# A hybrid decoder layer on one core: V and K products in eight steps of two K tiles, and modulation weights moved from the U products to the output projection

## The reference, cut to what matters

```python
m = silu(c) @ w_ada + b_ada              # 2048 x (6 * 2048): shift, scale, gate, shift2, scale2, gate2
h = rms_norm(x, g_pre) * (1.0 + scale) + shift
q, k, v, u = split(h @ w_in)             # 2048 -> 4 * 1024
attn   = diff_attend(rotary(q), rotary(k), v)        # samples also read pages of a cache
pooled = pool_mix(u)                     # window means minus u, times w_pool
mix = concat([rms_norm(attn) * 0.8, pooled]) @ w_out
x = x + gate * rms_norm(mix, g_post)
f = square(relu((rms_norm(x, g_pre2) * (1 + scale2) + shift2) @ w_ff1)) @ w_ff2
x = x + gate2 * rms_norm(f, g_post2)
```

## Time and profile before

| | us |
|---|---|
| median of 3 runs | 1502.26 (1497.86 to 1507.72) |
| the profiled execution | 1494.64 |
| its span, first to last instruction | 1493.0 |
| PE busy in the span | 1446.6 (97%) |
| DVE, ACT, POOL busy | 799.7, 517.5, 102.9 |
| first product matmul | 43.73 |
| first matmul of Q (fill 0) | 198.7 |
| first matmul of the output projection | 410.6 |

### The profile page before, as it was taken

How to read it: one execution, slowest core, us unless ns; L and a number is a source line. 1 busy time by engine, 2 the same in 40 slices (tenths; PEclk the granted TensorE clock), 3 DMA queues, 4 the chain that set the end, 5 groups by cost and what they waited for, 6 DMA issues and landing times.

```text
span 1493.0 us, 26969 instructions
## 1 busy us (share of the span) xinstructions
PE 1446.6 (97%) x10274; PEld 1313.3 (88%) x10274; DVE 799.7 (54%) x1258; ACT 517.5 (35%) x733; POOL 102.9 (7%) x177
## 2 busy tenths in 40 slices
PE   5999999999899998999999999999999999999996
PEld 1777777778588877999998999999999999999996
DVE  2655558856756568665334444333554344445554
ACT  2222233434456445333322333332333232333331
POOL 1000000067410000000000000000000000000002
PEclk9999999999999999999999999999999999999998
DMA  9999988889687777444445544445544444444431
GB/s 366 345 326 323 325 305 318 284 308 360 226 321 257 258 256 248 141 152 158 143 160 200 176 160 148 147 162 185 192 158 144 157 151 141 143 155 152 141 113 71
DMA packets 87880, 316.40 MB, mean 212 GB/s; under 512 B 12176, under 2 KB 12432, under 8 KB 87168
## 3 DMA queue, kind: packets, MB, share of 16 engines
q1 hardware_dynamic: 79200, 287.87, 56.1%
q0 software_dynamic: 5216, 22.51, 4.1%
q10 hardware_dynamic: 3392, 5.01, 0.9%
HBM read 309.56 MB, written 5.80 MB: 211 GB/s over the span
## 4 chain that ended last, share of the span: by engine, by line
PE 83%; DMA 6%; DVE 3%; POOL 2%; issue 2%; ACT 2%; POOLq 1%; SPq 0%; DVEq 0%; ACTq 0%
PE bank L1538 69%; PE bank L1609 7%; DMA raw<-in_stream 4%; PE bank L1500 3%; PE bank L1515 2%; DMA k_pages<-in_kc 1%; DMA pools_out<-u 1%; DMA pool_w<-in_w_pool 1%; ACT w_hi L390 1%; DVE w_lo L782 1%; PE bank L1861 1%; POOLq L1377 0%; POOL win L1396 0%; POOL win L1398 0%; ACT pair L639 0%
## 5 line engine op out<-in xcount | busy, mean ns | idle before, releaser
L390 ACT ACTIVATE w_hi<-raw 128x1024 fp32r<-128x1024 f32 x352 | 361.8, 1054 | 352.8 <-PE bank L1538 232.8
L782 DVE TENSOR_TENSOR w_lo<-raw,w_hi 128x1024 fp32r<-128x1024 f32 x352 | 419.6, 1225 | 117.1 <-ACT w_hi L390 114.9
L1538 PE MATMUL bank<-m_hi,w_hi 128*128 128x320 f32 x1280 | 397.4, 310 | 1.0 <-issue 0.6
L1538 PE MATMUL bank<-m_hi,w_lo 128*128 128x320 f32 x1280 | 395.5, 309 | 0.0
L1538 PE MATMUL bank<-m_lo,w_hi 128*128 128x320 f32 x1280 | 395.5, 309 | 0.0
L1538 PE MATMUL bank<-h_hi,w_hi 128*128 128x320 f32 x1216 | 379.2, 312 | 0.0
L1538 PE MATMUL bank<-h_hi,w_lo 128*128 128x320 f32 x1216 | 375.7, 309 | 0.0
L1538 PE MATMUL bank<-h_lo,w_hi 128*128 128x320 f32 x1216 | 375.7, 309 | 0.0
L1538 PEld LDWEIGHTS bank<-m_hi,w_hi 128*128 128x128 f32 x1280 | 240.3, 188 | 15.0 <-issue 15.0
L1538 PEld LDWEIGHTS bank<-h_hi,w_hi 128*128 128x128 f32 x1216 | 228.2, 188 | 23.2 <-issue 23.2
L1538 PEld LDWEIGHTS bank<-m_lo,w_hi 128*128 128x128 f32 x1280 | 240.3, 188 | 0.0
(11 more groups left out here) (237 smaller groups left out, 1095.3 us busy)
## 6 DMA issues: line engine op xcount, KB each, us to landing
raw<-in_stream SPq DMA_DIRECT2D x544, 512.0 KB, 5.0
k_pages<-in_kc POOLq DMA_DIRECT2D x16, 512.0 KB, 9.3
v_pages<-in_vc POOLq DMA_DIRECT2D x16, 512.0 KB, 6.9
x<-in_x_cm ACTq DMA_DIRECT2D x1, 2560.0 KB, 12.2
x<-in_x_cm POOLq DMA_DIRECT2D x1, 2560.0 KB, 10.8
v_out<-v_cm POOLq DMA_DIRECT2D x1, 1280.0 KB, 9.5
k_out<-back POOLq DMA_DIRECT2D x1, 1280.0 KB, 10.2
y_out<-x SPq DMA_DIRECT2D x2, 640.0 KB, 3.0
```

The costliest lines, as they stand in the source:

```text
L390: act.activation(w_hi[2 * (j % 2) + h][:, :], raw[slot][:, h * 1024:(h + 1) * 1024], ACT.Copy).then_inc(hi_ready, 1)
L782: dve.tensor_tensor(w_lo[q][:, :], raw[slot][:, h * 1024:(h + 1) * 1024], w_hi[q][:, :], ALU.subtract).then_inc(slot_used[slot], 1)
L1538: last = pe.matmul(bank[j % 2][:, 0:T], w[q][:, k * P:(k + 1) * P], v[:, 8 * h + k, :], start=(h == 0 and k == 0 and n == 0), stop=(h == 1 ...
```

## The change

The number of chunks stays 272, and every weight is used as often as before; what changes is the order.

- x is loaded first, in four parts, on SyncE's queue; ACT no longer loads it. PE makes the mean square before the ada chunks.
- An ada block below 8 holds scale and shift of two K tiles instead of one of both for four. So one block (4 chunks) stands ahead of the V and K stage instead of two.
- V and K are made in 8 steps of two K tiles. A product chunk holds eight output tiles, and a bank collects 6 matmuls instead of 12. Scale and shift of the prompt tokens are one ACT instruction a tile; POOL's and DVE's parts are of two tiles. ACT's and DVE's loops are written out.
- U has no ada chunks (PLAIN). The first 12 tiles of the output projection have two each (DENSE), the last four one (SUPER): 28 in that stage instead of 16.
- scale2 is thus ready only after tile 5 (OUT_SCALE); DVE makes it there (`make_scale2`), and x and the projection are scaled two tiles at a time after it.

Where the names in the rows below are: `raw_49` to `raw_52` are the four slots, `w_hi_53` to `w_hi_56` and `w_lo_57` to `w_lo_60` the four halves; 9x512 is an ada matmul, 128x320 a product matmul or an eviction of 320 tokens.

The diff, cut to its core:

```diff
-STREAM = 8 + 12 * QUARTERS + 12 * Q_GROUPS + 8 * (U_GROUPS + OUT_GROUPS) + 36 * GROUPS
+SLICES = 2 * QUARTERS
+OUT_DENSE, OUT_PART = 3, 4
+OUT_SCALE = (KT - OUT_PART) // 2 - 1
+STREAM = 4 + 12 * (QUARTERS + Q_GROUPS) + 4 * U_GROUPS + 8 * OUT_GROUPS + 4 * OUT_DENSE + 36 * GROUPS
+SLICED = [0, 3, 6, 9]
+SLICED_ADA = [[1, 2, 4, 5], [7, 8, 10, 11]]
 DENSE = [2, 5, 8, 11]
-DENSE_ADA = [[0, 1, 3, 4], [6, 7, 9, 10]]
+NORMED = [(0, 2), (2, 4), (4, 8), (8, 12), (12, 16)]
...
     def out_use(n):
-        return 2 + 3 * (QUARTERS + Q_GROUPS) + 2 * (U_GROUPS + n)
+        return quarter_use(QUARTERS + Q_GROUPS) + U_GROUPS + 2 * n + min(n, OUT_DENSE)
 
...
+    def out_chunk(n):
+        return OUT_C4 + n // 4, out_use(n // 4), (DENSE if n // 4 < OUT_DENSE else SUPER)[n % 4], n % 4
...
+        if f < 16:
+            n = f // 4 - 2
+            return U_C4 + n, quarter_use(QUARTERS + Q_GROUPS) + n, PLAIN[f % 4], f % 4
+        return out_chunk(0)
...
+        first = 2 * (n - OUT_SCALE - 2)
+        return (first, first + 1) if 0 <= first < KT else ()
+    def m_parts(n):
+        def until(n):
+            return max(0, min(n + 1, 2 * (n - OUT_SCALE + 1)))
+        return range(until(n - 1), until(n)) if n < KT - 1 else ()
...
+        for g in range(4):
+            sp.dma_start(x[:, 4 * g:4 * g + 4, :], x_cm[:, 4 * g:4 * g + 4, :]).then_inc(x_loaded[g], 16)
...
-        act.dma_start(x[:, :, :], x_cm).then_inc(x_loaded, 16)
...
+            for k in range(2):
+                tile = normed[:, 2 * n + k, 0:NP_]
+                act.activation(tile, tile, ACT.Identity, bias=mod[:, n, 2 + k, 0:1], scale=gate[:, 2 * n + k, 0:1]).then_inc(
+                    prompt_mod, 1)
+            act.wait_ge(prompt_mod, 2 * n + 2)
+            act.wait_ge(sample_mod, n + 1)
+            act.activation(h_hi[:, 2 * n:2 * n + 2, :], normed[:, 2 * n:2 * n + 2, :], ACT.Copy).then_inc(h_hi_s, 1)
...
+        for n in range(SLICES):
+            second, following = slice_chunks(n)
+            for h in range(2):
+                hi_half(*second, h)
+            ada_copy(n + 1, quarter_use(n // 2), SLICED_ADA[n % 2][3])
+            hi_half(*following, 0)
+            if n + 1 < SLICES:
+                slice_h(n + 1)
+            hi_half(*following, 1)
...
+                if n == OUT_SCALE:
+                    act.wait_ge(gate_done, SLICES + 2)
+                for m in m_parts(n):
+                    scale_m(m)
...
+        def slice_gate(n):
+            mod_add(n)
+            dve.wait_ge(mod_done, n + 2)
+            dve.scalar_tensor_tensor(gate[:, 2 * n:2 * n + 2, :], mod[:, n, 0:2, :], 1.0,
+                                     gain[:, G_PRE_MIX + 2 * n:G_PRE_MIX + 2 * n + 2].unsqueeze(2).to_broadcast([P, 2, NSEQ]),
                                      ALU.add, ALU.mult).then_inc(gate_done, 1)
...
-            dve.wait_ge(gate_done, q + 1)
-            part = normed[:, tiles, 0:NP_]
-            mine.mark(dve.tensor_tensor(part, part, gate[:, tiles, 0:1].to_broadcast([P, 4, NP_]), ALU.mult))
...
+            half = 4 * n + 2 * jj + h
+            for i in range(4):
+                if i < 3:
+                    dve.wait_ge(first_done, 3 * half + i + 1)
                 else:
-                    dve.wait_ge(half_free, 8 * g + (2 * j + h + 5))
-                n, b = 4 * (j % 2) + 2 * h + i, 2 * h + i
-                tile = v_cm[:, n, :] if j < 2 else k_cm[:, n, :]
-                dve.tensor_tensor(tile, QUARTER_BANKS[b][:, 0:T], tile, ALU.add).then_inc(bank_free[b], 1)
-        def quarter(g, following, more):
+                    dve.wait_ge(half_free, half + 5)
+                tile = (v_cm, k_cm)[jj][:, 4 * h + i, :]
+                dve.tensor_tensor(tile, QUARTER_BANKS[i][:, 0:T], tile, ALU.add).then_inc(bank_free[i], 1)
...
+        for n in range(SLICES):
+            second, following = slice_chunks(n)
+            for h in range(2):
+                lo_half(*second, h)
+                sum_tiles(n, 0, h)
+            if n + 1 < SLICES:
+                slice_gate(n + 1)
+            else:
+                mod_add(n + 1)
+            lo_half(*following, 0)
+            sum_tiles(n, 1, 0)
+            if n + 1 < SLICES:
+                low_of_h(n + 1)
+            lo_half(*following, 1)
+            sum_tiles(n, 1, 1)
...
+        def make_scale2():
+            mod_part(0, out_use(OUT_SCALE // 4), DENSE[OUT_SCALE % 4] - 1)
+            dve.wait_ge(part_done, 1)
+            dve.scalar_tensor_tensor(scale2[:, :, :], mod_of(SCALE2), 1.0,
+                                     gain[:, G_PRE_FFN:G_PRE_FFN + KT].unsqueeze(2).to_broadcast([P, KT, NSEQ]),
+                                     ALU.add, ALU.mult).then_inc(gate_done, 1)
...
+                if 4 * t + j == OUT_SCALE:
+                    make_scale2()
...
+            part = seq_view(normed[:, 2 * n:2 * n + 2, NP_:T])
+            mine.then(pool.tensor_tensor(part, part, bcast_seq(gate[:, 2 * n:2 * n + 2, :]), ALU.mult))
+            pool.tensor_tensor(part, part, bcast_seq(mod[:, n, 2:4, :]), ALU.add).then_inc(sample_mod, 1)
...
-        for a in range(3):
+        sum_parts(0)
+        mean_of_parts(0)
+        for a in range(4):
             ada_chunk(0, 0, a, a)
-        sum_parts(0)
-        ada_chunk(0, 0, 3, 3)
-        mean_of_parts(0)
         pe.wait_ge(tables_loaded, 48)
         ada_turn(0)
-        for a in range(4):
-            ada_chunk(1, 1, a, a)
-        ada_turn(1)
+        keep_clock(bank[5], 8)
...
+            def slice_tiles(i, jj, h, tiles):
+                j = 2 * i + jj
+                slot, u = use_of(use, SLICED[j])
+                q = 2 * (j % 2) + h
+                pe.wait_ge(slot_used[slot], 2 * u + (3 + h))
+                for b in tiles:
+                    pe.wait_ge(bank_free[b], 8 * g + (2 * j + h + 1))
+                    for k in range(2):
+                        for n, (w, v) in enumerate(((w_hi, h_hi), (w_hi, h_lo), (w_lo, h_hi))):
+                            last = pe.matmul(QUARTER_BANKS[b][:, 0:T], w[q][:, (2 * b + k) * P:(2 * b + k + 1) * P],
+                                             v[:, ds(4 * g + (2 * i + k), 1), :].rearrange("p a t -> p (a t)"),
+                                             start=(k == 0 and n == 0), stop=(k == 1 and n == 2))
+                    last.then_inc(first_done if b < 3 else half_free, 1)
+            for i in range(2):
+                nb, places = 2 * g + (i + 1), SLICED_ADA[i]
+                ada_chunk(nb, use, places[0], 0)
+                pe.wait_ge(h_ready, 2 * g + (i + 1))
+                slice_tiles(i, 0, 0, range(4))
+                ada_chunk(nb, use, places[1], 1)
+                ada_chunk(nb, use, places[2], 2)
+                slice_tiles(i, 0, 1, range(2))
+                ada_chunk(nb, use, places[3], 3)
+                slice_tiles(i, 0, 1, range(2, 4))
+                ada_turn(nb)
+                slice_tiles(i, 1, 0, range(4))
+                slice_tiles(i, 1, 1, range(2))
+                if last and i == 1:
+                    nb, place, a = fill_ada(0)[0][0]
+                    ada_chunk(nb, fill(0)[1], place, a)
+                slice_tiles(i, 1, 1, range(2, 4))
...
-        for t in range(OUT_GROUPS - 1):
+        for n in range(4 * OUT_DENSE):
+            c4, use, off, j = out_chunk(n)
+            for i in range(2):
+                k = OUT_PART + 2 * n + i
+                ada_part_chunk(k // KT, use, off - 2 + i, k % KT, k == KT)
+            for h in range(2):
+                product_half(c4, use, off, j, h, m_hi, m_lo, mix_wait)
+        for t in range(OUT_DENSE, OUT_GROUPS - 1):
...
+MOD_TILES = [[(part, 2 * n + k) for part in (1, 0) for k in range(2)] for n in range(SLICES)]
+MOD_TILES += [[(part, 4 * n + k) for k in range(4)] for part in (2, 4, 3, 5) for n in range(4)]
```

More of the change, by code:

```diff
@@ L60 @@
 FFN_C4 = OUT_C4 + OUT_GROUPS
-BANK_LEAD = 4 * QUARTERS - 2 * Q_C4
+BANK_LEAD = 8 * QUARTERS - 2 * Q_C4
 U_ORDER = [6, 7, 4, 5, 2, 3, 0, 1]
@@ L292, in fill_ada, with normed_by @@
         if f < 8:
-            nb = 10 + 2 * (f // 4) + j // 2
+            nb = 9 + f // 2
             return [(nb, off - 2, 2 * (j % 2)), (nb, off - 1, 2 * (j % 2) + 1)], nb if j % 2 else None
-        nb = 14 + f // 4 - 2
-        return [(nb, off - 1, j)], nb if j == 3 else None
+        return [], None
+    def normed_by(n):
+        return sum(1 for first, _ in NORMED if first <= 2 * n)
     def seq_view(ap):
@@ L407, in freed, with slice_h @@
             ins.then_inc(bank_free[j % 2], 1)
-        square_all(x, x_loaded, lambda g: 16)
+        square_all()
         copy_parts(0)
         root(bank[5][:, 0:T], 1, KT / 4)
-        ada_copy(0, 0, 3)
[L414 to L419, removed]
-            act.activation(h_hi[:, ds(first, 4), :], normed[:, ds(first, 4), :], ACT.Copy).then_inc(h_hi_s, 1)
-        h_hi_part(1, 0)
-        for h in range(2):
-            hi_half(0, quarter_use(0), DENSE[0], 0, h)
+        def slice_h(n):
+            act.wait_ge(gate_done, n + 1)
```

(21 more changed lines are left out.)

236 lines of the change are left out of this document (71 added, 165 removed).

## The result

The changed kernel is slower, by a little: 1505.61 us median of 20 runs against 1497.39 us for the kernel before over 20 runs beside it, ratio 1.0048 [1.0034, 1.0062], so +7.2 us where I had forecast -8.5. Both are within 1% of no change, but the sign was wrong. The time itself lies just inside my range of 1483 to 1506, and that is luck: I had built the range on the median of three runs, 1502.26, and the 20 runs beside the changed kernel have 1497.39. As a difference the range was -19 to +4 us, and +7.2 is outside it. One of the 20 runs took 4952.74 us; nothing here explains it, and the median doesn't feel it. The profiled execution has a span of 1500.4 us against 1493.0, so the two traces hold the whole difference (7.4).

The account below looks back on a forecast made before the run. PE was taken to set the pace after a DMA-bound start. Terms -15.4 + 0.6 + 0.5 - 5.8 - 0.2 + 11.8 = -8.5, so 1502.26 - 8.5 = 1493.8 us by the median of the runs; range 1483 to 1506.

Parts of the forecast that it names:

- Start: Up to the first V and K product: fewer bytes loaded ahead, first product at 28.3 instead of 43.73, gain 15.4 us.
- V and K: First product to Q: one more ada chunk and a wait in the first step, loss 0.6 us.
- I put no other wait on the new steps: V and K: beyond the 1.1 us in the first step, the seven later steps of 19.2 us add no wait.
- the slack of 0.6 us behind the turn: V and K: PE wants bank 0 again after 3.7 us; DVE's work until then takes 3.1 with semaphores.
- Rival E: PE waits for its banks in all eight V and K steps; at 2.5 us each +11.5, 1513.8 us; chance 0.10.
- The first step: V and K: its third ada chunk waits for a slot and for queued bytes, loss 1.1 us.
- U: U without ada chunks: eight at 0.98 are 7.8 us of PE, less 1.0 and 1.0 for waits, gain 5.8.
- Q: Q stage: one turn more lies inside it, 0.43 us, loss 0.5.
- the pooled tile: Output projection: the wait for the last pooled tile is now covered by the second ada chunk, gain 0.2 us.
- the 11.8: Output projection: twelve more ada chunks at 0.98 us, which nothing hides, loss 11.8 us.
- So it fits, with 1.5 to spare: Output projection: the next product chunk has 9.2 us to land, be rounded and subtracted; its first half needs 7.7.
- D: Output projection bound by the stream at 327 GB/s, tiles of 9.62 us: -3.3 in all, 1499.0 us; chance 0.10.

Follow-up runs that it names:

- e1: The changed kernel, but in the last V/K step DVE evicts both halves of K before subtracting the first Q chunk: 1499.25 us, 1.0011 of the kernel before.
- e5: The changed kernel, but in dense projection tiles PE multiplies one ada chunk between the halves of the tile before: 1502.63 us, 1.0044 of the kernel before.
- e7: The changed kernel with the edits of e1 and e5 and the reload of x in four parts: 1491.45 us, 0.9968 of the kernel before.
- e4: The changed kernel, but three of four matmuls of the first ada chunk of each dense projection tile left out: 1506.71 us, 1.0055 of the kernel before.
- e8: The changed kernel with the edit of e1 and the reload of x in four parts, without that of e5: 1495.58 us, 0.9982 of the kernel before.

## Why the prediction was wrong

**Start: right.** The first product came at 29.15, where I had 28.3.

**V and K: "I put no other wait on the new steps" failed at one step of eight.** For the steps that I worked out it held: later steps start 18.9 to 19.3 us apart, 19.0 in the mean, against my 19.2, PE waits for no eviction in them, and the slack of 0.6 us behind the turn was enough. Rival E was wrong. But I worked out one step and used it for the last one as well. There the "following" chunk of DVE and ACT is Q's, two ada chunks deeper in the stream, and DVE's order makes the evictions wait for it: 4.7 us and 1.5 of slow matmuls. e1 took both away with DVE's order alone. The listing in front showed the order `w_lo`, then eviction; I had counted its time and not asked when its chunk lands at the seam. The first step lost 2.8 instead of 1.1: its fourth ada chunk's second half took 5.45 us from issue to landing, to 36.28.

**U: right in size**, -4.9 against -5.5 with Q and the pooled tile, though the second ada chunk of the first projection tile (1.0) is in the -4.9 and not in the -5.5. PE waited 2.7 us for the key pages instead of 1.3, and no longer for `pool_w`; these nearly cancel.

**Projection: the 11.8 was near, the sentence "So it fits, with 1.5 to spare" failed.** Two chunks in a row cost 1.83 and not 1.96, so the eleven more of this stage cost 9.4. Beyond them came 10.8 us of waits and of slow work behind them. 6.8 at the second tile: I named the stream's need for a steady tile and never listed what else is issued in the first one. There the reload of x, 2.6 MB, shares the DMA engines with the two chunks that the second tile needs, and the four slots hold only one product chunk with DENSE, where SUPER had two. With the 408 GB/s of the earlier trace rows, x and these two chunks are (2.62 + 2 x 1.05) / 0.408 = 11.6 us on the way, where the tile had 9.1; so the sum would have shown a wait. In the trace it is longer still: x is issued at 397.4, and the product chunk's first half is there at 411.9. The remaining 4 are the waits of 2.33 and 1.69 in the steady tiles. I had taken the loop of V and K (7.7 us) over, where ada chunks are used between halves and the loads leave one by one. With two in a row the product chunk is issued right behind another. Ahead of the two waits its first half was on its way for 8.7 and 8.1 us alone, and from the free slot to the first product, for which I had 7.7, the fifth tile took 432.6 to 444.2, 11.5 us. e5 shows it: with the ada chunks between halves as in V and K, the same half takes 5.0 to 6.4 us from the fourth tile on, and the waits are gone.

The Trainium skill's figure of about 358 GB/s from HBM ("DMA: Bandwidth & Descriptors", "Where 436 GB/s comes from"), which I set aside for the 408 of the earlier trace rows, is near the most that a projection moved over a long stretch: 362 GB/s over 94 us in e7, with the DMA engines 0.98 busy. PE hardly waited there, so this is a rate that was reached and not shown to be a limit; shorter stretches were faster, 413 GB/s from 400 to 405 us in the changed kernel. Even by the figure of 358 the tile of 9.1 us fits (346 GB/s), so it names no failed step. D gave the nearest time of my rivals to the tiles, 9.62 us, by the wrong mechanism.

In sum: +6.2 at the seam, +6.8 at the second tile and +4.0 after it are 17.0; the start and the first V and K step add 2.5; that two ada chunks in a row cost 0.12 less than two apart, in eight steps and eleven tiles, takes off 2.3, and smaller terms 1.3. -8.5 + 15.9 = +7.4, the difference of the two traces, against 7.2 by the runs.

## What to carry to other kernels

When a loop's step is worked out, work out the step at its seam too: ask for each instruction in front of an eviction when its input lands there, and put what waits for a transfer behind what frees a bank. Where prefetch goes through a few slots in fixed order, the kinds of chunks in it decide the depth. Chunks that only the slowest engine frees are better used one at a time where the loop would wait otherwise (here each change of matmul kind had a price, and e5 alone gained nothing), and a bulk load should not be issued just where the mix of chunks changes. Moving work off a loaded stage pays only if what stands in the other one is still fed.

## What the hardware showed that I had not expected

- The four matmuls of an ada chunk, into four groups of a bank's rows, take the time of one: 1.81 us for two chunks with three matmuls left out, 1.83 with all eight (e4).
- PE's granted clock fell behind waits: to 0.50, the lower level of 1.2 GHz, in 184.50 to 187.00 us of the changed kernel behind the wait of 4.67, where matmuls follow each other every 0.267 us instead of every 0.147 at full clock. It fell behind some shorter waits too and not behind others: in e8 48 matmuls took 8.81 us behind a wait of 1.95, and 7.27 behind one of 2.13. It added 1.5 us to the wait of 4.67, and in the profile of e1 2.7 (10.01 instead of 7.28 us for 48 matmuls) at the projection's second tile.
- Changing between ada chunks and products costs about 0.15 us each time (an estimate, 0.32 us a tile for two changes more): two ada chunks are 0.98 + 0.98 apart against 1.83 in a row, two halves 2 x 3.71 against 7.23 (e5).

The stretches of the changed kernel at the lower level, at the end of V and K and at the projection's second tile (columns as in the earlier trace rows, PEclk third from the end):

```profile
184.50:187.00 2.50, 2.50 (x10) 2.50 (x11) 2.45 (x5) 0.00 (x0) 0.00 (x0) 0.50 0.02 7
409.40:412.70 3.30, 3.12 (x8) 0.18 (x8) 0.00 (x0) 0.74 (x1) 0.00 (x0) 0.50 1.03 421
```
